# The last layer norm of a decoder step: the shift by the mean as a matmul of two rows

## The reference

```python
def _layernorm(x, g, b):
    xf = x.astype(jnp.float32)
    mu = jnp.mean(xf, -1, keepdims=True)
    var = jnp.mean(jnp.square(xf - mu), -1, keepdims=True)
    return ((xf - mu) * lax.rsqrt(var + LN_EPS) * g + b).astype(x.dtype)
...
    x2 = _layernorm(ALPHA * x1 + hdn @ lp['w_down'], lp['ln2_g'], lp['ln2_b'])
```

## Time and profile before

| | us |
|---|---|
| median of 3 runs | 2748.62 (2745.72 to 2748.69) |
| the profiled execution, its own time | 2749.74 |
| its span in the trace | 2747.7 |
| TensorE busy | 2679.2 |
| VectorE busy | 1625.2 |
| ScalarE busy | 1163.3 |
| first to last operation that makes y_prompt's output (lines 2598, 2601) | 2733.07 to 2744.80 |

### The profile page before, as it was taken

One profiled execution on the slowest core, in us unless ns is written; L12 is line 12 of the kernel. 1 busy time (PEld: TensorE's weight loads), 2 busy tenths in 40 slices (PEclk: granted clock), 3 DMA queues, 4 the chain that ended last, 5 costly groups with the idle time before them and its releaser, 6 DMA issues.

```text
span 2747.7 us, 55700 instructions
## 1 busy us (share of the span) xinstructions
PE 2679.2 (98%) x23575; PEld 2620.8 (95%) x23575; DVE 1625.2 (59%) x1770; ACT 1163.3 (42%) x1460; POOL 0.2 (0%) x4
## 2 busy tenths in 40 slices
PE   7999999999999999999999999999999999999997
PEld 7988899999999999999999998988999999999997
DVE  5566547788554545555586575577964545545444
ACT  4445333456333333333354453344653333333332
POOL 0000000000000000000000000000000000000000
PEclk9999999999999999999999999999999999999998
DMA  7544334466666666556664543353666666665653
GB/s 230 175 122 121 95 93 145 134 180 184 178 183 177 182 179 180 177 184 178 183 201 140 173 121 93 86 163 104 201 189 179 176 185 180 181 179 185 207 179 114
DMA packets 280390, 447.43 MB, mean 163 GB/s; under 512 B 45174, under 2 KB 76336, under 8 KB 279928
## 3 DMA queue, kind: packets, MB, share of 16 engines
q1 hardware_dynamic: 278600, 441.59, 54.1%
q10 hardware_dynamic: 1618, 3.31, 0.4%
HBM read 433.06 MB, written 11.78 MB: 162 GB/s over the span
## 4 chain that ended last, share of the span: by engine, by line
PE 89%; DVE 7%; ACT 2%; issue 2%; ACTq 0%; DMA 0%; DVEq 0%; SPq 0%
PE psum L700 19%; PE psum L702 19%; PE psum L701 19%; PE psum L733 6%; PE psum L734 6%; PE psum L735 6%; DVE w_lo L1762 2%; PE psum L930 1%; PE psum L723 1%; ACT w_hi L1327 1%; PE psum L724 1%; PE psum L725 1%; PE psum L1101 1%; PE psum L1086 1%; PE psum L1090 1%
## 5 line engine op out<-in xcount | busy, mean ns | idle before, releaser
L1758 DVE TENSOR_TENSOR w_lo<-w_raw,w_hi 128x1024 fp32r<-128x1024 f32 x496 | 606.1, 1225 | 680.3 <-ACT w_hi L1314 679.2
L1314 ACT ACTIVATE w_hi<-w_raw 128x1024 fp32r<-128x1024 f32 x504 | 533.7, 1060 | 886.8 <-PE psum L702 861.3
L700 PE MATMUL psum<-x_hi,w_lo 128*128 128x264 f32 (+3 forms) x3072 | 877.7, 286 | 2.1 <-DVE x_lo L2087 1.0
L701 PE MATMUL psum<-x_lo,w_hi 128*128 128x264 f32 (+3 forms) x3072 | 874.8, 285 | 0.0
L702 PE MATMUL psum<-x_hi,w_hi 128*128 128x264 f32 (+3 forms) x3072 | 874.3, 285 | 0.0
L700 PEld LDWEIGHTS psum<-x_hi,w_lo 128*128 128x128 f32 x3072 | 579.4, 189 | 3.4 <-issue 1.3
L701 PEld LDWEIGHTS psum<-x_lo,w_hi 128*128 128x128 f32 x3072 | 580.7, 189 | 0.2
L702 PEld LDWEIGHTS psum<-x_hi,w_hi 128*128 128x128 f32 x3072 | 579.5, 189 | 0.0
L1762 DVE TENSOR_TENSOR w_lo<-w_raw,w_hi 128x1024 fp32r<-128x1024 f32 x304 | 368.0, 1223 | 205.6 <-ACT w_hi L1327 189.1
L1327 ACT ACTIVATE w_hi<-w_raw 128x1024 fp32r<-128x1024 f32 x292 | 304.1, 1054 | 272.1 <-PE psum L735 194.5
L733 PE MATMUL psum<-x_hi,w_lo 128*128 128x264 f32 (+1 forms) x1376 | 411.4, 299 | 5.1 <-ACT p_tail L1350 2.1
(11 more groups left out here) (501 smaller groups left out, 2515.0 us busy)
## 6 DMA issues: line engine op xcount, KB each, us to landing
w_raw<-in_w_in SPq DMA_DIRECT2D x192, 512.0 KB, 3.8
w_raw<-in_w_gate SPq DMA_DIRECT2D x176, 512.0 KB, 3.8
w_raw<-in_w_up SPq DMA_DIRECT2D x176, 512.0 KB, 4.2
w_raw<-in_w_down SPq DMA_DIRECT2D x176, 512.0 KB, 3.7
w_raw<-in_w_out SPq DMA_DIRECT2D x64, 512.0 KB, 4.3
w_raw<-in_w_in SPq DMA_DIRECT2D x16, 262.0 KB, 2.9
r_sample<-in_state_ret SPq DMA_DIRECT2D x6, 512.0 KB, 8.0
out_s_ret<-r_sample SPq DMA_DIRECT2D x6, 512.0 KB, 6.4
```

The costliest lines, as they stand in the source:

```text
L700: mm(out, w1, bh[:, k, 0:nt], start=(k == 0), stop=False)
L701: mm(out, w0, bl[:, k, 0:nt], start=False, stop=False)
L1314: A(wh[:, j, :, :], raw[:, j, :, :], ACT.Copy).then_inc(S.hi_ready, 1)
L1758: TT(wl[:, j, :, :], raw[:, j, :, :], wh[:, j, :, :].bitcast(F32), ALU.subtract).then_inc(S.lo_ready, 1)
```

## The change

The last norm is written as y = (x g) r + (-m r) g + b. The product x g (helper `gained`) is made in place in `Y`: for the first three groups after slabs 48, 68 and 80, for columns 1536 to 1791 after the addition of block 14, for the last 256 columns after the reciprocal. The statistics are made of x before that, in pieces of 256 and 128 columns, the last one straight from PSUM. The second part is a matrix product with a contraction over two rows: `yrow` holds the rows (-m r) and 1 for the 256 tokens, `gain_rows` the rows g and b. VectorE writes -m r into `ymr` beside a column of ones, TensorE transposes `ymr` twice into [2, 256], ScalarE copies it to `yrow`, and `shifted(i)` makes the product for piece i in PSUM bank 4 + i % 4. VectorE then does one operation for each piece, with the PSUM bank as its last operand. For pieces 4 to 7 TensorE waits until VectorE has read the bank. The sample rows' two sums and the turn of their columns are placed between these products; their last two operations stand before piece 7, and so does their store. The two rows of `gain_rows` are loaded by two more DMAs; the broadcast loads of g and b stay.

```diff
@@ -305,10 +305,13 @@
...
-    ycol = at("y_columns", P_LN + T * 4, [128, 40, 2])
-    yst = ycol[:, 0:30, :].rearrange("p a b -> p (a b)").rearrange("p (t k) -> p t k", t=2)
-    ymv, ysd, yroot = ycol[:, 30:32, :], ycol[:, 32, :], ycol[:, 33, :]
-    sm1, nms, sm2, sds = (ycol[:, 34 + i, 0:1] for i in range(4))
+    ycol = at("y_columns", P_LN + T * 4, [128, 46, 2])
+    yst = ycol[:, 0:36, :].rearrange("p a b -> p (a b)").rearrange("p (t k) -> p t k", t=2)
+    ymv, ysd, yroot = ycol[:, 36:38, :], ycol[:, 38, :], ycol[:, 39, :]
+    sm1, nms, sm2, sds = (ycol[:, 40 + i, 0:1] for i in range(4))
+    ymr = ycol[:, 44:46, :]
+    yrow = over_x("y_mean_rows", 8 * D + 1024, [2, 256])
+    gain_rows = at("y_gain_rows", F_SG, [2, D])
...
@@ -662,15 +665,16 @@
                             for i, name in enumerate(('ln2_g', 'ln2_b')):
                                 row_ = a[name][l].rearrange("(o d) -> o d", o=1).to_broadcast([128, D])
                                 sp.dma_start(gains[:, i, :], row_).then_inc(S.start_loaded, 16)
-            for t in range(2):
-                for q in range(4):
-                    sp.wait_ge(S.ln_folded, 2 * DEPTH + 4 * t + q + (2 if 4 * t + q > 4 else 1))
-                    sp.dma_start(o['y_prompt'][0, 128 * t:128 * t + 128, GC * q:GC * q + GC], Y[:, t, GC * q:GC * q + GC]).then_inc(S.y_stored, 16)
-                    if 4 * t + q == 4:
-                        sp.wait_ge(S.ln_folded, 2 * DEPTH + 6)
-                        sp.dma_start(o['y_sample'][:, 0, :].rearrange("s (b c) -> b s c", c=128), ysm[:, :]).then_inc(S.y_stored, 16)
+                                sp.dma_start(gain_rows[i:i + 1, :], a[name][l].rearrange("(o d) -> o d", o=1)).then_inc(S.start_loaded, 16)
+            for i in range(8):
+                if i == 7:
+                    sp.wait_ge(S.ln_folded, 2 * DEPTH + 8)
+                    sp.dma_start(o['y_sample'][:, 0, :].rearrange("s (b c) -> b s c", c=128), ysm[:, :]).then_inc(S.y_stored, 16)
+                t, c = i // 4, GC * (i % 4)
+                sp.wait_ge(S.ln_folded, 2 * DEPTH + i + (2 if i == 7 else 1))
+                sp.dma_start(o['y_prompt'][0, 128 * t:128 * t + 128, c:c + GC], Y[:, t, c:c + GC]).then_inc(S.y_stored, 16)
...
@@ -1291,13 +1295,31 @@
             pe.wait_ge(S.ln_scaled, 10 * DEPTH + 4)
             pe.wait_ge(S.y_rows, 5)
             turn(15, 2, 1).then_inc(S.y_turned, 1)
+            pe.wait_ge(S.start_loaded, 128)
+            def shifted(i):
+                if i >= 4:
+                    pe.wait_ge(S.ln_folded, 2 * DEPTH + i - 3)
+                mm(ps[:, 4 + i % 4, :], yrow[0:2, 128 * (i // 4):128 * (i // 4) + 128], gain_rows[0:2, GC * (i % 4):GC * (i % 4) + GC],
+                   start=True, stop=True).then_inc(S.y_turned, 1)
+            pe.wait_ge(S.ln_centered, 8 * DEPTH + 1)
+            for t in range(2):
+                last = tr(ps[0:2, 1, 256 + 128 * t:384 + 128 * t], ymr[:, t, :], ident)
+            last.then_inc(S.y_turned, 1)
+            pe.wait_ge(S.y_rows, 8)
+            shifted(0)
+            shifted(1)
             pe.wait_ge(S.ln_scaled, 10 * DEPTH + 5)
-            pe.wait_ge(S.y_rows, 6)
             tr(ps[:, 0, 128:256], rsm[:, :], ident).then_inc(S.y_turned, 1)
-            pe.wait_ge(S.start_loaded, 96)
+            shifted(2)
+            shifted(3)
             for i, x in enumerate((sm1, sm2)):
                 pe.wait_ge(S.ln_sum, 2 * DEPTH + 2 + i)
                 mm(ps[:, 1, 128 + i:129 + i], mod8[:, :], x, start=True, stop=True).then_inc(S.ln_sum_all, 1)
+                shifted(4 + 2 * i)
+                shifted(5 + 2 * i)
 
 
         @block.scalar
@@ -1721,15 +1743,21 @@
                             last = A(gains_s[:, :, :].rearrange("p a f -> p (a f)"), ps[:, 2, 0:256], ACT.Copy)
                         last.then_inc(S.y_rows, 1)
                     own(A(yroot, eps[:, 0:2], ACT.Sqrt))
-            for n in range(4):
-                act.wait_ge(S.y_turned, 4 + n)
+            def last_rows(n):
                 c = 3 * GC + 128 * n
-                for t in range(1 if n == 3 else 2):
+                for t in range(2):
                     last = A(Y[:, t, c:c + 128], ps[:, 2 * (n % 2) + t, 0:128], ACT.Copy)
                 last.then_inc(S.y_rows, 1)
+            for n in range(3):
+                act.wait_ge(S.y_turned, 4 + n)
+                last_rows(n)
             act.wait_ge(S.ln_sum, 2 * DEPTH + 1)
             A(ysd, ymv[:, :, 1], ACT.Sqrt, bias=eps[:, 0:1]).then_inc(S.ln_std, 1)
+            last_rows(3)
             act.wait_ge(S.y_turned, 8)
+            A(yrow[0:2, :], ps[0:2, 1, 256:512], ACT.Copy).then_inc(S.y_rows, 1)
+            act.wait_ge(S.y_turned, 11)
             A(ysm[:, :], ps[:, 0, 128:256], ACT.Copy).then_inc(S.y_rows, 1)
             act.wait_ge(S.ln_sum_all, 2 * DEPTH + 1)
             own(A(nms, ps[:, 1, 128:129], ACT.Copy, scale=-1.0 / D))
@@ -2545,6 +2573,13 @@
 
             s, g0 = slab0(DEPTH - 1, 'down'), group0(DEPTH - 1, 'down')
             l = DEPTH - 1
+            def gained(c0, c1):
+                for t in range(2):
+                    last = TT(Y[:, t, c0:c1], Y[:, t, c0:c1], gains[:, 0, c0:c1], ALU.mult)
+                own(last)
+            own(v.memset(ymr[:, :, 1], 1.0))
             for k in range(4, 4 * DOWN_SLABS, 4):
                 lo4(s + k, (3,) if k == 44 else range(RING))
                 if k == 40:
@@ -2566,49 +2601,55 @@
                 if k in (48, 68, 80):
 
                     q = (48, 68, 80).index(k)
+                    if q == 0:
+                        dve.wait_ge(S.start_loaded, 128)
                     dve.wait_ge(S.y_rows, q + 1)
                     for t in range(2):
-                        v.bn_stats(yst[:, t, 6 * q:6 * q + 6], Y[:, t, GC * q:GC * q + GC])
+                        ins = v.bn_stats(yst[:, t, 6 * q:6 * q + 6], Y[:, t, GC * q:GC * q + GC])
+                    own(ins)
+                    gained(GC * q, GC * q + GC)
             for n in range(4):
                 dve.wait_ge(S.slab_used, s + YB + n + 1)
                 Rb = R[:, 12 + n, :]
                 TT(Rb, Rb, ps[:, 4 + n, 0:T], ALU.add).then_inc(S.ln_scaled, 1)
-            dve.wait_ge(S.ln_scaled, 10 * DEPTH + 4)
-            v.tensor_copy(rsm[:, :].rearrange("p (b s) -> p b s", s=NS), R[:, :, SEQ:T]).then_inc(S.ln_scaled, 1)
+                if n == 2:
+                    dve.wait_ge(S.y_rows, 5)
+                    for t in range(2):
+                        ins = v.bn_stats(yst[:, t, 18:24], Y[:, t, 3 * GC:3 * GC + 256])
+                    own(ins)
+                    gained(3 * GC, 3 * GC + 256)
             dve.wait_ge(S.y_rows, 6)
             for t in range(2):
-                v.bn_stats(yst[:, t, 18:24], Y[:, t, 3 * GC:3 * GC + 384])
+                v.bn_stats(yst[:, t, 24:30], Y[:, t, 3 * GC + 256:3 * GC + 384])
             dve.wait_ge(S.y_turned, 7)
-            own(v.tensor_copy(Y[:, 1, 3 * GC + 384:], ps[:, 3, 0:128]))
-            v.bn_stats(yst[:, 1, 24:30], Y[:, 1, 3 * GC + 384:])
-            dve.wait_ge(S.y_rows, 7)
-            own(v.bn_stats(yst[:, 0, 24:30], Y[:, 0, 3 * GC + 384:]))
+            for t in range(2):
+                ins = v.bn_stats(yst[:, t, 30:36], ps[:, 2 + t, 0:128])
+            own(ins)
             for t in range(2):
                 last = v.bn_aggr(ymv[:, t, :], yst[:, t, :])
             last.then_inc(S.ln_sum, 1)
-            dve.wait_ge(S.y_rows, 8)
-            v.tensor_reduce(sm1, ysm[:, :], AX.X, ALU.add).then_inc(S.ln_sum, 1)
+            dve.wait_ge(S.ln_scaled, 10 * DEPTH + 4)
+            v.tensor_copy(rsm[:, :].rearrange("p (b s) -> p b s", s=NS), R[:, :, SEQ:T]).then_inc(S.ln_scaled, 1)
             dve.wait_ge(S.ln_std, 2 * DEPTH + 1)
             own(v.reciprocal(ysd, ysd))
-            dve.wait_ge(S.start_loaded, 96)
-            before = None
-            for i in range(9):
-                if i < 8:
-                    y, g = Y[:, i // 4, GC * (i % 4):GC * (i % 4) + GC], gains[:, :, GC * (i % 4):GC * (i % 4) + GC]
-                    made = own.mark(STT(y, y, ymv[:, i // 4, 0:1], g[:, 0, :], ALU.subtract, ALU.mult))
-                if i:
-                    dve.wait_ge(S.dve_steps, before[0])
-                    STT(before[1], before[1], before[2], before[3][:, 1, :], ALU.mult, ALU.add).then_inc(S.ln_folded, 1)
-                before = (made, y, ysd[:, i // 4:i // 4 + 1], g) if i < 8 else None
-                if i == 2:
+            STT(ymr[:, :, 0], ymv[:, :, 0], -1.0, ysd, ALU.mult, ALU.mult).then_inc(S.ln_centered, 1)
+            dve.wait_ge(S.y_rows, 7)
+            gained(3 * GC + 256, 4 * GC)
+            for i in range(8):
+                t, c = i // 4, GC * (i % 4)
+                dve.wait_ge(S.y_turned, (9, 10, 12, 13, 14, 15, 16, 17)[i])
+                STT(Y[:, t, c:c + GC], Y[:, t, c:c + GC], ysd[:, t:t + 1], ps[:, 4 + i % 4, :], ALU.mult, ALU.add).then_inc(S.ln_folded, 1)
+                if i == 1:
```

(6 more changed lines are left out.)

## The result

The changed kernel takes 2756.05 us (median of 10 runs, 2751.39 to 2757.65), the one before 2748.8 (10 runs, 2745.72 to 2752.09). The ratio is 1.0022, its 95% interval 1.0014 to 1.003 (3.8 to 8.2 us): slower, by about the 0.2% that can be told from no change. The prediction had 2747.1 us, in a range that ended at 2751.2, and gave 14% to the case that came true.

The account below looks back on a forecast made before the run. The stream of weight products on TensorE was taken to bound the kernel almost everywhere, VectorE its tail. New tail -3.2 us, low clock +1.7, together -1.5: from 2748.62 to 2747.1 us, range 2743.2 to 2751.2.

Parts of the forecast that it names:

- What bounds the tail: After the last weight product: eight f32 products on TensorE, 0.86 us each, set the time; -3.2 us at the upper clock.
- The statistics: From the last addition to the first new product at 2732.90: statistics and preparation together last as long as the statistics before.
- The moved work: After slabs 48, 68 and 80, x g under the weight products: cost 0, up to 1.1 us at each of two places.
- The clock: In the tail: it falls just before the products and is low for 3.4 us, +1.7 us, giving -1.5 us.
- Rival 3: In the tail: the clock stays low to the end, as two-row products may not bring it back; +3.8 us, 14%.
- Same: Whole kernel: 0.92 for no change that can be told, as no case alone reaches 5.5 us; faster 0.04, slower 0.04.
- Those 2.9 us I leave as they are: From VectorE's end to the end of the span, with the last store: taken as unchanged at 2.9 us.
- theory B: Set up after the result, for the tail: products using two of 128 rows neither hold the clock up nor bring it back.

Follow-up runs that it names:

- filled gap: The changed kernel with 15 fp32r products in TensorE's gap before the two transposes and 3 before the first two-row product; ratio to the kernel before 1.0014.
- one pass: The changed kernel with both operands of the two-row products in fp32r instead of f32, without the broadcast load of b; ratio to the kernel before 0.9984.

## Why the prediction was wrong

*What bounds the tail.* Right: the products on TensorE, not VectorE, and for the reason given, two instructions of 0.43 us at the upper level for a plain f32 matmul. At 0.50 the measured pairs take 1.72 us. By the Trainium skill's isolated gap of 216 ns for 512 columns (TensorE: Matmul & The Clock Gate, Back-to-back issue gap) VectorE would, as an estimate, have stayed the bound; for this dtype the traces have 0.86 us a product at 1.00 and 1.72 at 0.50, and they decide.

*The statistics.* Right within 0.25 us: aggregation 2.05 us after the last addition began (2.07 in the sum), first product 3.89 us (3.66). The transposes took 0.53 instead of 0.44.

*The moved work.* Right: one plane at each of the two places 0.9 us late instead of 1.1, nothing on TensorE. The fourth addition was on time, the 256-column work done 0.95 us before it.

*The clock: the step that failed.* "I take 3.4 us low, the shorter case with its edges." The fall was foreseen, with its place. That it ends was taken from two stretches of other work: from 162.9 products over 64 rows, taking both halves of the rows in turn (line 930), from 435.7 mostly products over all 128. No row had products of two rows. Rival 3 named exactly that, but I gave it 14%, because TensorE would be busy without a gap. The runs show otherwise: with two rows the clock fell after 3.1 us of uninterrupted work (filled gap), and with 2, 32 and 64 rows it stayed low for 16 us, while with 128 it was back 6.8 us after its fall. Low from 2733.3 to the end costs 7.0 us by the prediction's own working, instead of 1.7.

The trace of the kernel before had a warning, in a row that the prediction used only for its 6.7 us. At 435.6 the clock fell with no idle time ahead of it (a row of the timeline, then windows of TensorE):

```profile
435.80 1.00 PE L1173 MATMUL psum<-p_rw,rw_sample 64*64 64x1 f32 x16
...
434.00:435.00 1.00, 1.00 (x40) 1.00 0.00 0
435.00:436.00 1.00, 1.00 (x34) 0.82 0.00 0
436.00:437.00 1.00, 1.00 (x17) 0.50 0.06 16
```

TensorE was busy for all of these microseconds, with 128 products of line 1173 from 432.4 on, one column each, over 64 rows. "TensorE is busy without a gap here" was thus no ground for taking 3.4 us instead of the whole tail.

*The size of rival 3.* It said +3.8 us; the tail is 5.4 longer. The sixteen instructions with the three pieces between them and the drain were summed to 15.0 us (13.8 + 0.2 + 0.8 + 0.2) and took 16.34. About 0.9 of this lies in the groups: what follows one starts 3.70 us after its first instruction and not 4 x 0.86 = 3.44, and the last ends with its drain (3.77), 14.9 in all instead of 14.0. The other 0.4 lies in the pieces between, 0.41, 0.52 and 0.52 us instead of 1.0 in all. The start was 0.2 late: 3.8 + 1.3 + 0.2 = 5.3, and 5.4 were measured.

*Same, faster, slower.* "Same" at 0.92 rested on no case reaching 5.5 us alone. The tail's 5.4 and the 0.6 behind it make 6.0 us, 0.22%, the measured ratio. That the two agree so well is partly luck, with an interval of 3.8 to 8.2 us; the rest of the 7.25 us between the medians lies within what both kernels scatter. The 0.6 us were a term at nothing in the prediction ("Those 2.9 us I leave as they are").

That 128 zero rows undo the loss, that one pass removes it with two rows and a low clock, and that the gap filled alone removes only part of it (3.05 of 5.4 us), leaves theory B with a product length of two instructions as the shown cause. Why 64 rows left the clock low in this tail, when 128 did not and line 930 with 64 did not either, stays open.

## What to carry to other kernels

A matmul with a contraction of two rows is not a small matmul: it streams as long as one of 128 (3.77 and 3.78 us for two products at 0.50), in plain f32 as two instructions, and here it ran at half the clock for as long as only such products followed. Where operands can be split, put the high parts and remainders into more rows of one fp32r product: five rows in one pass cost about 0.44 us at the low clock (1.21 for two, less a drain of 0.33) where two rows in f32 cost 1.72. And a price read from rows at the upper clock level must be read again for the state in which the new work will start, and for whether that work itself can lift it.

## What was not expected of the hardware

Zero rows matter: padding the contraction from 2 to 128 rows with zeros, same instructions and same columns, took the tail from 21.0 to 15.75 us. With 32 and 64 rows it stayed at 20.9, although products over 64 rows of both halves in turn had the clock back by 166.0 elsewhere in the kernel.

The profiled executions differ by 3 to 5 us long before the tail. The last addition of a block stands at 2724.9 to 2725.7 us in five of them and at 2729.2 to 2730.3 in the seven others, each of another kernel. The times of one kernel fall apart likewise: those of one pass are 2742.0 to 2742.5 us in four executions and 2745.3 to 2747.6 in seven. The time at 0.50 up to 2720 us, summed from windows of 10 us, is 20.4 us in each of the five early ones and 27.2 to 30.8 in the seven late ones. 6.8 us more at half the clock cost 3.4 us, most of that difference.
